# Products that nothing reads, placed in TensorE's waits of a decoder step's sample tile

## What is computed

```python
p = h @ w_in                       # split among three groups of heads
A: multi-head latent attention     # low-rank q and kv, paged cache for the samples
B: RWKV-7 time mixing, 4 heads of 64:
   S = S*(diag(w) - kk^T (a*kk)) + v k^T ;  y = S r
C: gated causal convolution of width 3
h = LN(alpha*h + concat(A, B, C) @ w_out)
h = LN(alpha*h + HierMoE(h))       # top-1 of 4 groups, top-2 of 8 experts
```

## Time and profile before

| | us |
|---|---|
| median of 3 runs | 3750.14 (3747.36 to 3765.46) |
| the profiled execution | 3730.53 |
| its span, first to last instruction | 3728.5 |
| TensorE busy | 3242.1 (87%) |
| DVE / ACT / POOL busy | 1274.4 / 912.9 / 584.4 |
| mean granted clock | 0.907 |

### The profile page before, as it was taken

One profiled execution on the slowest core, in us unless ns is written; L12 is line 12 of the kernel. 1 busy time (PEld: TensorE's weight loads), 2 busy tenths in 40 slices (PEclk: granted clock), 3 DMA queues, 4 the chain that ended last, 5 costly groups with the idle time before them and its releaser, 6 DMA issues.

```text
span 3728.5 us, 54744 instructions
## 1 busy us (share of the span) xinstructions
PE 3242.1 (87%) x22252; PEld 2008.2 (54%) x22252; DVE 1274.4 (34%) x3192; ACT 912.9 (24%) x1913; POOL 584.4 (16%) x587
## 2 busy tenths in 40 slices
PE   7997888998889979999499878899898999699990
PEld 3445667777666544333244566777767755334330
DVE  4103444444443351111341134444434434411116
ACT  0001233434442101111110113334434321011111
POOL 1000011111100013343300001111111000243333
PEclk9995899999999989999699869899989899799995
DMA  6112122222213229994721211222221132599826
GB/s 251 53 39 64 44 76 76 76 76 73 73 54 114 86 81 404 408 416 174 280 88 39 83 33 62 76 76 76 76 71 51 50 125 78 215 386 414 349 80 225
DMA packets 168757, 519.40 MB, mean 139 GB/s; under 512 B 41472, under 2 KB 82368, under 8 KB 143168
## 3 DMA queue, kind: packets, MB, share of 16 engines
q0 software_dynamic: 65600, 337.74, 23.6%
q1 hardware_dynamic: 83328, 106.86, 9.2%
q10 hardware_dynamic: 19584, 71.31, 4.9%
HBM read 630.21 MB, written 86.89 MB: 192 GB/s over the span
## 4 chain that ended last, share of the span: by engine, by line
PE 75%; DVE 9%; DMA 7%; ACT 4%; issue 2%; DVEq 2%; POOL 0%; ACTq 0%; SPq 0%; POOLq 0%
PE ps L770 65%; PE ps L767 10%; DMA w_slots<-in_w_gu,rowA 4%; DVE grams L2126 2%; DMA c_x<-xd 1%; DVE S_all L2524 1%; ACT PT L1863 1%; DVE PT L2547 1%; DVE c_x L2162 1%; DMA c_b<-ybd,dga 0%; ACT S_all L1832 0%; ACT kT L1591 0%; ACT PT L1591 0%; DMA xb<-xd,idall 0%; DVE t L2126 0%
## 5 line engine op out<-in xcount | busy, mean ns | idle before, releaser
L770 PE MATMUL ps<-w_slots,xbT 128*64 128x512 f32 (+1 forms) x2048 | 468.4, 609 | 27.3 <-DMA w_slots<-in_w_gu,rowA 23.4
L770 PE MATMUL ps<-hT,w_in 128*128 128x512 f32 x896 | 390.6, 597 | 3.2 <-ACT hT L1591 3.2
L770 PEld LDWEIGHTS ps<-w_slots,xbT 128*64 128x64 f32 x2048 | 175.0, 140 | 276.7 <-issue 261.8
L770 PE MATMUL ps<-grams 128*128 128x128 f32 (+1 forms) x2448 | 294.2, 276 | 29.5 <-DVE grams L2126 23.1
L770 PEld LDWEIGHTS ps<-grams 128*128 128x128 f32 (+1 forms) x2448 | 272.1, 188 | 51.0 <-issue 28.0
L770 PEld LDWEIGHTS ps<-hT,w_in 128*128 128x128 f32 x896 | 170.9, 192 | 216.1 <-issue 211.0
L770 PE MATMUL ps<-w_out,o_mixT 128*128 128x512 f32 x576 | 260.9, 600 | 1.3 <-DVE o_h L2745 1.3
L1591 ACT ACTIVATE kT<-ps 128x512 f32<-128x512 f32 x320 | 188.1, 596 | 254.4 <-PE ps L767 252.4
L770 PE MATMUL ps<-w_slots,hidT 128*64 128x512 f32 (+1 forms) x1024 | 233.9, 598 | 1.2 <-ACT hidT L1591 1.2
L2914 DVE SCALAR_TENSOR_TENSOR gt<-gt,ps 128x256 f32<-128x256 f32 x64 | 26.9, 421 | 517.8 <-ACT gt L2071 517.8
L767 PE MATMUL ps<-cst,S_all 128*128 128x128 f32 x832 | 159.9, 311 | 20.3 <-ACT PT L1591 20.3
(11 more groups left out here) (376 smaller groups left out, 5139.8 us busy)
## 6 DMA issues: line engine op xcount, KB each, us to landing
ybd<-yb ACTq DMA_DIRECT2D x64, 512.0 KB, 8.3
pd<-stage SPq DMA_DIRECT2D x56, 256.0 KB, 2.5
out_y<-c_h ACTq DMA_DIRECT2D x27, 512.0 KB, 2.9
w_in<-in_w_in SPq DMA_DIRECT2D x6, 2048.0 KB, 25.4
o_mixT<-mixd SPq DMA_DIRECT2D x18, 512.0 KB, 3.5
o_h<-out_y SPq DMA_DIRECT2D x18, 512.0 KB, 4.7
xd<-o_x ACTq DMA_DIRECT2D x18, 512.0 KB, 2.8
c_x<-xd ACTq DMA_DIRECT2D x18, 512.0 KB, 6.8
```

What stands on the lines that cost most here:

```text
L770: return pe.matmul(out, lhsT, rhs, start=start, stop=stop, skip_group_check=True)
```

## The change

A helper `fill(n)` issues n products of the identity with the first 512 columns of the constants into `Q[3]`. Nothing reads them, they wait for nothing and raise nothing. They are placed between the steps of the sample tile (27 per layer), between the heads of `u_sample` (3), in `st_sample` (11) and in the seam that follows the sample tile (10): 51 per layer.

```diff
--- before.py
+++ after.py
@@ -769,6 +769,11 @@
             def mm(out, lhsT, rhs, start, stop):
                 return pe.matmul(out, lhsT, rhs, start=start, stop=stop, skip_group_check=True)
 
+            def fill(n):
+
+                for _ in range(n):
+                    mm(Q[3], ident, cst[:, 0:512], True, True)
+
             def transposed_rows(l, t):
 
                 W = P if t < NPT else WS
@@ -1088,6 +1093,8 @@
                         f, s = h // 2, 64 * (h % 2)
                         for b in range(NB):
                             m = mm(by_pair(K01, 64)[:WS, h % 2, f, :], swT[s:s + 64, f, b, :], stS[s:s + 64, b, f, :], b == 0, b == NB - 1)
+                        if h < RH - 1:
+                            fill(1)
                     self.done(m, "u0")
 
                 def st_sample(self):
@@ -1103,6 +1111,8 @@
                             dst = ps[s:s + 64, 2048 + 128 * b + 64 * f:2112 + 128 * b + 64 * f]
                             mm(dst, sbk[:, 0, b, 64 * h:64 * h + 64], uu[:WS, 64 * h:64 * h + 64], True, False)
                             m = mm(dst, sbk[:, 1, b, 64 * h:64 * h + 64], tokm[:WS, f, s:s + 64], False, True)
+                            if b == 3 or b == 7 and h < RH - 1:
+                                fill(1)
                     self.done(m, "st0")
 
                 def mixT(self):
@@ -1282,6 +1292,8 @@
 
             def seam(x, y, b):
 
+                if not b:
+                    fill(6)
                 y.lora()
                 b.pnT()
                 b.pt(3)
@@ -1289,39 +1301,62 @@
                 b.v(3)
                 b.pt(1)
                 b.v(0)
+                if not b:
+                    fill(3)
                 x.mixT()
                 b.pt(2)
                 b.v(1)
+                if not b:
+                    fill(1)
                 y.mlaT()
                 b.v(2)
                 y.kks()
 
             def sample_tile(l):
                 x = Tile(l, NPT)
+                fill(3)
                 x.lora()
+                fill(2)
                 x.mlaT()
+                fill(1)
                 x.kks()
                 x.q()
                 x.kkb()
+                fill(1)
                 x.qlat()
+                fill(1)
                 x.qrT()
+                fill(2)
                 x.new()
                 x.tokm()
+                fill(1)
                 x.gramD()
                 x.gram23()
+                fill(1)
                 x.sq(0)
                 x.gram4()
+                fill(1)
                 x.rr(0)
+                fill(1)
                 x.sq(1)
+                fill(1)
                 x.rr(1)
+                fill(1)
                 x.sq(2)
+                fill(1)
                 x.rr(2)
+                fill(1)
                 x.off1()
+                fill(1)
                 x.off2()
                 x.mv()
+                fill(1)
                 x.off3()
+                fill(1)
                 x.wt()
+                fill(1)
                 x.u_sample()
+                fill(5)
                 x.st_sample()
                 seam(x, Tile(l, 0), NoTile())
```

## The result

The changed kernel takes 3782.4 us (median of 10 runs, 3772.0 to 3801.1) against 3750.1 us (10 runs, 3744.4 to 3765.5): ratio 1.0094, 95% interval 1.0079 to 1.0109. It is slower, 30 to 41 us, where +13 us and "no change that can be told" were forecast. The profiled execution of the changed kernel took 3795.1 us, that of before 3730.5: the first is among the longest of its runs and the second is shorter than any of the ten, so the 65 us between these two traces exaggerate.

The account below looks back on a forecast made before the run. TensorE at its lower clock was taken to bound most of the sample tile, DVE elsewhere. Nine terms summed to +6.3 us per layer, +13 for two layers: 3763 us beside the 3750.1 median, range 3738 to 3784.

Parts of the forecast that it names:

- wt to u: wt products and the wait before u: the wt products shorten, the one added product hides; -1.3 us per layer.
- the seam: Stretch after the sample tile: the added products fit its waits and DVE mostly sets the end; 0 us per layer.
- rival A: Whole changed tile: filled waits hold the clock high throughout; -8.7 us per layer, 3733 us; chance 0.08.
- rival B: State products: the clock comes back one head late in each layer; 3774 us; chance 0.31.
- C: Whole changed tile: added products don't move the clock at all; +62 us per layer, 3874 us; chance 0.03.
- the price of one added product: Every added 128x512 product: 0.87 us at full clock, from 448 projection products, and 1.71 at the lower clock.
- The five behind u: Five added products between u and the state products: between 4.3 and 8.6 us, taken as 6.2.
- For the narrow products of u and the state I take 0.5: u and state products: at the higher clock their time falls by a factor 0.5.
- Start to `new`: Tile start through q to the `new` products: 0 up to the latent rows, then +1.0 us per layer.
- `new` to the first squaring: Scores and transposes halve, less the product added behind the transposes; -1.0 us per layer.
- item 6: u with its three products and the five behind: starts at the lower clock; +10.2 us per layer, lowered from +10.8.
- slot 0: q of slot 0, after the seam: most of it stays at the lower clock; -0.4 us per layer.

Follow-up runs that it names:

- no_five: The changed kernel without the five added products behind u; those in u and in the state products stay: 3799.8 us (one run).
- moved_before_u: The changed kernel with its five products behind u moved into the wait before u, six there in all: 3791.2 us (6 runs), ratio 1.0103.

## Why the prediction was right or wrong

**What held.** The place and the order of things: the clock at 1.00 into q (until 296.3, where 293 was written), then 0.50 for the most part until 310, 1.00 in the gram steps, 0.50 in u until inside the five products, 1.00 in the state products. wt to u (-1.3, measured -1.0) and the seam (0, +0.3 and +0.5) were right. So was the bound of rival A: even at full clock the added work finds too few waits. That its sum came out beyond rival B's 3774 us is not B's doing: in the profiled runs of the changed kernel the state products run at 1.00 from their first head on. B's mechanism exists (`no_five`, the long runs of `moved_before_u`), but it wasn't seen in either profile of this kernel. C is out.

**The step that failed** is the price of one added product, "0.87 us each at full clock", with 1.71 at the lower one, and the same mistake in what the cut streams cost: both were taken as rates out of a dense row and put to single pieces. Per layer, against the forecast:

- A product between others takes 1.06 us, not 0.87: 9 in the gram steps and 11 in the state products make 20 x 0.19 = 3.8 us. At the lower clock it takes 2.01, not 1.71: the three in u, 0.9 us.
- The five behind u took 7.3 us, not 6.2: +1.1.
- u in four pieces takes 7.3 us (1.81 and three times 1.84) at the lower clock where the row of before gave 5.7: +1.6. The forecast counted the products put in and not what cutting a stream in four does to the stream.
- "For the narrow products of u and the state I take 0.5": a head of the state takes 6.65 - 3 x 1.06 = 3.5 us at full clock and not 3.0, so 4 x 0.5 = +2. The gram steps' groups take 0.62 us from start to start, not 0.52, +0.9 in all.

This is 10.3 of the 15.4 us by which a layer missed. The rest has other causes:

- Start to `new` was set to +1.0 between -2.6 and +6: measured +3.9 and +3.7. The clock fell at 296.3, and the product behind kkb, that behind qlat and the two behind qrT ran at 0.50: +2.8. This is the place of a fall and not a price.
- `new` to the first squaring, set to -1.0, took +0.1: the scores went from 3.87 to 2.81 us at full clock and weren't halved, and the product behind the transposes ran at 0.50. +1.1.
- The correction of item 6 downwards ("I allow for an earlier rise") had no row behind it and made it worse by 0.6. wt to u and the seam missed by 0.3 each.

What was taken from the trace as a duration was right; what was taken as a rate out of a dense stream (0.87 from 448 products in a row, 5.74 for 64 records in a row) and put to single pieces was too low each time. Two rows of the same trace, 483.36 and 342.45, had 1.06 and 1.84.

**Luck in the number.** Two layers at 15.4 us would be 31 us over the forecast, and the median is only 19 over. In the second profile of the changed kernel the two tiles are 19.5 and 16.7 us longer than before, and its two slots 0 together some 5 us shorter, where the forecast had -0.4 a layer: 31 us in all, as the medians say. So falls of the clock at other places and a shorter slot 0, neither of them forecast, took back part of the miss. The range held the time only at its edge, 3782 of 3784.

**The baseline.** The profile that the sum was made against was a short execution, 0.5% under the median. That did little harm to the sums, since the tile is the same to 0.2 us in both profiles of before, but the two traces alone would have put 30 us too much on the change.

## What to carry to other kernels

Price an inserted instruction at what it costs alone, between others of another kind, and count what it does to the stream that it cuts; here a rate from a dense loop was its lower bound. Look in the trace for an instance that already stands alone. Work added to keep a clock up paid here inside waits, ahead of a stretch that then kept the clock by itself for a while; on the path it cost more than it brought (15 us per layer in the state block). In the state products single insertions held the clock and didn't raise it, and needed a dense run ahead of them. Where that run stood before u, the result had two values from run to run: take several profiles before believing one.

## What the runs showed of the hardware

Two things were not expected. With the five products before u, the state block has two values in the same code, 39.9 us or 66.5, by whether the clock falls within u. The Trainium skill, "TensorE: Matmul & The Clock Gate", Part 1, says of the clock's rise at a kernel's start that it differs from run to run; these runs show that a fall in the middle of one does too, and that here it costs 27 us each time. And one execution differs from another in the prompt slots, whose code is the same in all these kernels: slots 1 to 7 of layer 0 took 703 us at a mean clock of 0.94 up to 724 at 0.91. These 20 us compare with a spread of 26 over the runs of the kernel before (3739 to 3765 us, its first profile apart).
